# One step's scores, maxima and sums put in another order in a global attention kernel

## The reference

```
def one_block(qblk):
    s = jnp.einsum('bkgqd,bksd->bkgqs', qblk, k).astype(jnp.float32) * scale
    p = jax.nn.softmax(s, axis=-1).astype(v.dtype)
    return jnp.einsum('bkgqs,bksd->bkgqd', p, v)
```

## Time and profile before

| | |
|---|---|
| time before, median of 3 runs | 3031.06 us (3029.05 to 3032.88) |
| the profiled execution | 3032.3 us |
| its span, first to last instruction | 3030.7 us |
| mean granted clock of TensorE | 0.973 of full speed |
| busy over the span: PE, DVE, ACT, POOL | 93%, 55%, 44%, 30% |
| `attend_global`, first scores to last `weigh` | 373.8 to 1079.9 us |

### The profile page before, as it was taken

One profiled execution on the slowest core, in us unless ns is written; L12 is line 12 of the kernel. 1 busy time (PEld: TensorE's weight loads), 2 busy tenths in 40 slices (PEclk: granted clock), 3 DMA queues, 4 the chain that ended last, 5 costly groups with the idle time before them and its releaser, 6 DMA issues. The chain is left out here.

```text
span 3030.7 us, 38875 instructions
## 1 busy us (share of the span) xinstructions
PE 2827.5 (93%) x12978; PEld 2318.1 (76%) x12978; DVE 1659.6 (55%) x2193; ACT 1329.4 (44%) x1882; POOL 910.1 (30%) x683
## 2 busy tenths in 40 slices
PE   7999499999999969979969999999999999999998
PEld 5888377777777738958858888888888888888887
DVE  5666388888888838855534432354224542254322
ACT  3222177777777738953323322244223432233221
POOL 1221189999999945532200000000001000010000
PEclk9999699999999979989979999999999999999999
DMA  5333611111111022348873343343434343343432
GB/s 174 107 107 98 159 25 32 30 29 34 27 34 29 18 78 79 83 139 206 235 215 98 97 147 90 110 134 97 151 90 134 109 125 118 93 151 97 122 94 83
DMA packets 473643, 308.96 MB, mean 102 GB/s; under 512 B 62451, under 2 KB 440579, under 8 KB 473148
## 3 DMA queue, kind: packets, MB, share of 16 engines
q1 hardware_dynamic: 443484, 274.46, 32.2%
q0 software_dynamic: 6496, 19.42, 2.0%
q10 hardware_dynamic: 23552, 13.64, 1.5%
HBM read 236.79 MB, written 66.40 MB: 100 GB/s over the span
## 5 line engine op out<-in xcount | busy, mean ns | idle before, releaser
L1686 DVE TENSOR_TENSOR f_w_lo<-f_w_raw,f_w_hi 128x1024 fp32r<-128x1024 f32 x256 | 313.8, 1226 | 864.3 <-ACT f_w_hi L1638 864.1
L1638 ACT ACTIVATE f_w_hi<-f_w_raw 128x1024 fp32r<-128x1024 f32 x256 | 271.4, 1060 | 980.4 <-PE f_down L122 553.1
L626 POOL TENSOR_TENSOR p_sum<-p_sum,p_hi 128x1024 f32<-128x1024 f32 x192 | 458.9, 2390 | 33.1 <-issue 25.1
L120 PE MATMUL f_up<-f_h,f_w_hi 128*128 128x512 f32 x1024 | 400.9, 391 | 19.7 <-DMA f_h<-h_split 19.7
L120 PE MATMUL f_down<-f_act_hi,f_w_hi 128*128 128x512 f32 x1024 | 401.2, 392 | 0.0
L122 PE MATMUL f_up<-f_h,f_w_lo 128*128 128x512 f32 x1024 | 399.8, 390 | 0.0
L121 PE MATMUL f_up<-f_h,f_w_hi 128*128 128x512 f32 x1024 | 399.8, 390 | 0.0
L122 PE MATMUL f_down<-f_act_hi,f_w_lo 128*128 128x512 f32 x1024 | 398.8, 389 | 0.0
L121 PE MATMUL f_down<-f_act_lo,f_w_hi 128*128 128x512 f32 x1024 | 398.3, 389 | 0.0
L679 DVE TENSOR_REDUCE part_max<-m_ps 128x1 f32<-128x1024 f32 x251 | 306.8, 1222 | 116.9 <-PE m_ps L724 116.9
L1614 POOL TENSOR_TENSOR f_rstd<-f_var,f_half 128x4 f32<-128x4 f32 x4 | 5.1, 1285 | 1186.3 <-DVE f_var L1706 1186.3
(11 more groups left out here) (202 smaller groups left out, 4841.3 us busy)
## 6 DMA issues: line engine op xcount, KB each, us to landing
f_w_raw<-in_w_ffn_up SPq DMA_DIRECT2D x128, 512.0 KB, 4.1
f_w_raw<-in_w_ffn_down SPq DMA_DIRECT2D x128, 512.0 KB, 3.8
f_h<-h_split SPq DMA_DIRECT2D x32, 512.0 KB, 5.7
x_in<-in_x SPq DMA_DIRECT2D x16, 512.0 KB, 4.2
q_split<-q_out ACTq DMA_DIRECT2D x16, 512.0 KB, 3.3
q_turned<-w_raw SPq DMA_DIRECT2D x16, 512.0 KB, 3.4
q_all<-q_turned SPq DMA_DIRECT2D x32, 256.0 KB, 3.3
wq_in<-q_split SPq DMA_DIRECT2D x32, 256.0 KB, 2.8
```

What stands on the lines that cost most here:

```text
L120: nc.tensor.matmul(out, stat_hi, mov_hi, start=first, stop=False)
L626: nc.gpsimd.tensor_tensor(p_sum[:, s], first, p_hi[:, (UNITS * n + u) % SLOTS].bitcast(F32), ALU.add).then_inc(added, 1)
L1638: nc.scalar.activation(w_hi[:, s], w_raw[:, s], ACT.Copy).then_inc(w_hi_made, 1)
L1686: nc.vector.tensor_tensor(w_lo[:, s], w_raw[:, s], w_hi[:, s].bitcast(F32), ALU.subtract).then_inc(w_lo_made, 1)
```

## The change

It does four things, all in `attend_global`.

1. TensorE issues the maxima products of a unit directly behind its scores, and `weigh` after both. VectorE reduces the maxima ahead of `low` in the same unit of its loop.
2. Of eight units' `p_hi`, GpSimd adds seven (six additions, `BY_ADDS`); the last unit's is summed by two TensorE products with a new matrix of ones, `ones_low`, in `weigh`.
3. The maxima products take 128 neighbouring query columns instead of every fourth one.
4. To match, `place_max` issues four DMAs of 128 values each instead of one.

```diff
-    ADDS = UNITS
+    BY_ADDS = UNITS - 1
+    ADDS = BY_ADDS
...
+        ones_low = sb("g_ones_low", [P, 2 * HD], F32R)
...
             def place_max(n):
                 sp.wait_ge(max_ready, n + 1)
-                sp.dma_start(q_max[HD:HD + 1, n % QS].bitcast(F32).rearrange("o (p t) -> o p t", t=QT), neg_max[:, n % 2].bitcast(F32)).then_inc(max_placed[n % 2], 16)
+                for t in range(QT):
+                    row = q_max[HD:HD + 1, n % QS, t * P:(t + 1) * P].bitcast(F32)
+                    sp.dma_start(row.unsqueeze(2), neg_max[:, n % 2, t:t + 1].bitcast(F32)).then_inc(max_placed[n % 2], 16)
...
-                for u in range(1, UNITS):
+                for u in range(1, BY_ADDS):
                     pool.drain()
...
-                if at >= SLOTS:
-                    before = at - SLOTS
+                before = at - SLOTS
+                if at >= SLOTS and before % UNITS < BY_ADDS:
                     act.wait_ge(added, ADDS * (before // UNITS) + max(before % UNITS, 1))
...
             for n in range(TOTAL):
                 for u in range(UNITS):
-                    if n > 0 or u > 0:
-                        low(n if u else n - 1, (u - 1) % UNITS)
                     ahead, m = pair_of(n, u)
                     if ahead < TOTAL:
                         reduce(ahead, m)
+                    if n > 0 or u > 0:
+                        low(n if u else n - 1, (u - 1) % UNITS)
...
-                    last = nc.tensor.matmul(bank[:, e], q_all[:, n % QS, t::QT],
+                    last = nc.tensor.matmul(bank[:, e], q_all[:, n % QS, t * P:(t + 1) * P],
...
                 last.then_inc(high_used, 1)
...
+                for e in range(2 if u >= BY_ADDS else 0):
+                    last = nc.tensor.matmul(ob_ps[:], ones_low[:], p_hi[:, slot, e * QB:(e + 1) * QB], start=False, stop=False)
...
                     scores(n, u)
-                    if at >= LAG:
-                        weigh((at - LAG) // UNITS, (at - LAG) % UNITS)
                     ahead, m = pair_of(n, u)
                     if ahead < TOTAL:
                         max_products(ahead, m)
+                    if at >= LAG:
+                        weigh((at - LAG) // UNITS, (at - LAG) % UNITS)
```

More of the change, by code:

```diff
@@ L606, in _ @@
             pool.drain()
-            nc.gpsimd.memset(ones_high[:, ONE_HIGH:], 1.0).then_inc(filled, 1)
+            nc.gpsimd.memset(ones_high[:, ONE_HIGH:], 1.0)
+            nc.gpsimd.memset(ones_low[:].bitcast(F32), 0.0)
+            pool.drain()
+            nc.gpsimd.memset(ones_low[:, ONE_LOW:ONE_HIGH].bitcast(F32), 1.0).then_inc(filled, 1)
             def combine(n):
@@ L684, in reduce @@
                     nc.vector.drain()
-                    at_least(dve, max_placed[n % 2], 16 * (n // 2))
+                    at_least(dve, max_placed[n % 2], 16 * QT * (n // 2))
                     nc.vector.tensor_scalar(neg_max[:, n % 2], row_max[:], -1.0, None, ALU.mult).then_inc(max_ready, 1)
@@ L731, in scores @@
                 if u == 0:
-                    pe.wait_ge(max_placed[n % 2], 16 * (n // 2 + 1))
+                    pe.wait_ge(max_placed[n % 2], 16 * QT * (n // 2 + 1))
                     pe.wait_ge(k_low_loaded[g], 16)
```

## The result

The changed kernel takes 3488.2 us (median of 4 runs, 3482.4 to 3496.5) against 3030.7 before: ratio 1.1515, 95% interval 1.1502 to 1.1528. It is 457 us slower. 3406 us were forecast, with a range that ends at 3480: the direction and the mechanism came out, the size was 82 us short.

A forecast was written before the change was run, and what follows sets the result against it. TensorE and VectorE were taken to wait for each other in a loop spanning two units, 22.05 us a step; the new order closes it every unit. 3031 + 363 (loop) + 15 (clock) + 2 (start) - 5 (end) = 3406 us, range 3360 to 3480.

The forecast's parts named there:

- The order closes a loop once per unit: In `attend_global`, scores, maxima products, reduction and low part follow one another: 4.14 us a unit, +363 us including unit 5.
- W: A unit's four weighing matmuls on TensorE, 0.92 us, forecast to lie beside VectorE's reduction and low part (2.42 us).
- TensorE's clock: +15 us: In `attend_global`, idle at unit 5 lowers the clock for a partial unit, 0.7 us, in two thirds of 31 steps.
- The first rival: Clock falls in regular units of `attend_global` too: low a third of the time, +99 us, 3490 us; chance 0.08.
- Unit 5: 0.81 us more: In unit 5 the row maximum and its negation precede the low part, adding 0.81 us to the loop 31 times.
- Costs put at nothing: In `attend_global`'s long loop: GpSimd's dropped addition, `ones_low` products, four placements per step and contiguous columns, each 0.
- The start: At the stage's start the first scores wait for three more placement DMAs: 0 to 6 us, taken as +2.
- the end: Behind the last ten units, the last matmul's wait for GpSimd's sum goes nearly whole: -5 us (0 to -6).
- The faster rival: In `attend_global`, GpSimd and waits were the bound; earlier maxima products leave VectorE's own work: 2956 us, chance 0.02.
- R: VectorE's reduction of a unit's maxima products; its start to the low part's start was forecast at 1.15 us.
- M: A unit's two maxima products on TensorE; their start to the reduction's start was forecast at 0.67 us.

The follow-up runs named there:

- the filled kernel: The changed kernel with four matmuls by a matrix of zeros added to each unit's `weigh`, its granted clock 1.00: 3394.6 us, ratio 1.1208.
- the short negation: The changed kernel with the negated maximum made by a reduction instead of a scalar product: 3444.0 us; with four matmuls by zeros per unit as well: 3387.6 us.

## Why the prediction was right in kind and short in size

- *The order closes a loop once per unit.* Right. 4.13 us for the unit shown against 4.14, and in the kernel whose clock never fell the stretch took 1038.7 us against 1041 forecast. Each order alone, put back, did what the loop says: VectorE's opened it, TensorE's put W into it.
- *TensorE's clock: +15 us.* This is the step that failed. The forecast let the clock fall only in unit 5, in two thirds of the steps and for part of a unit, and took the idle of 1.40 us in the earlier trace rows as a sign that a regular unit is safe. That was one idle with dense work on either side; in the new loop one comes every 4 us, and the clock also fell in regular units. The granted clock of 0.84 means 32% of the stretch at the low level. The measured price of the clock is 56 us with the short negation and 73 us (93 less 20) in the changed kernel. Of the 73 the two units behind unit 5 have 41, or 1.3 us a step where the forecast had 0.5, and units 0 to 4, where it had nothing, have 31. The price of one unit was right (5.38 - 4.13 = 1.25 us against 1.21); how often it is paid was not. Of the 246 units 59 begin with a matmul of over 0.6 us in place of 0.50, and 59 x 1.25 = 74 us, an estimate.
- *The first rival*, to which I gave 0.08, said a third of the time, +99 and 3490 us. Its mechanism and its third came true. That its time is met within 2 us is luck: its clock term is 26 us too high, and it has no negations.
- *Unit 5: 0.81 us more.* The row that it came from the earlier trace rows contains a negation of 0.49 us, read as its cost, while alone it takes 0.17. Where the negation met no addition, unit 5 took 4.67 us, 0.54 more than a regular unit. In the changed kernel the negation takes 0.93 in the mean, and that is 31 x (0.93 - 0.49) = 14 us of the missing 82, not counting the clock that the longer idle costs.
- *Costs put at nothing.* One addition moved from GpSimd: right in the loop, but the cover was not the only thing between GpSimd and VectorE, see the negations. Placement and layout: nothing in the long loop, right. The start was +0.4 instead of +2, and the end -3.7 instead of -5: small, as forecast.
- *The faster rival* needed R to start without waiting for M, and that did not happen: VectorE waited 504 us for it. Faster kernels came only where VectorE's order was put back, and then ended first at the placement and the negation.

By terms: loop 1041 - 678 = 363 forecast, 361 measured (1038.7 - 678.2, in the filled kernel, with its 9 us of negations in it); clock 15 forecast, 73 measured; further negations 0 forecast and 20 measured; ends -3 each. The measured terms are differences of the same few spans, so that they come to 450 again is no check of them; what tests the clock's term is the pair of kernels with the short negation.

## What to carry to other kernels

Before reordering two engines that hand work to each other, write down for each wait how many units back its producer lies: the change put a new waiter ahead of an old producer, and an overlap of two units became one loop of one. When a loop leaves TensorE idle in every round, price the low clock for regular rounds, not only for the longest gap, and take one survived gap for no proof. A reading of a short instruction's duration should be checked against its own shortest one, since a longer one may be a wait.

## What the hardware showed unexpectedly

- **More matmuls, less time.** 1024 matmuls by zeros took 94 us off, by holding the granted clock at 1.00 instead of 0.84 (and, for 20 us of it, by where the negations fell).
- **A VectorE instruction of four elements that waits for GpSimd.** The scalar product from SBUF to SBUF took 170 ns at least and 2158 at most, and the long one shown ended with a GpSimd addition. The reduction in its place took 156 to 158 ns in all 32 cases. This fits the Trainium skill, "SBUF — State Buffer", section Who interferes with whom: a scalar operation in its two-port mode and GpSimd exclude one another for a whole instruction, a reduction never does. The trace agrees in both: 930 against 157 ns in the mean, and 2.12 us beside a 2.34 us addition. Which mode the short operation ran in no run here shows.
- **Four small placements cost what they issue.** They take 2.53 us of SP's queue in place of 0.60, and this is on the path only where the step is short.
